# A blocked delta-rule recurrence on one core: two heads kept in halves of the partitions

## The chip, the cores and the metric

The kernel is one program on one core of a Trainium2 chip. The time is that of the device, in microseconds, from the start of the program to its end. TensorE (PE, with its weight loads as PEld), VectorE (DVE), ScalarE (ACT), GpSimd (POOL) and SyncE (SP) run their own instruction streams and meet at semaphores.

## What is computed

Two layers of a block with an RWKV-like recurrence, a convolution branch and a retrieval of experts (PEER), over 256 tokens of 1024 channels and a context of 256 tokens, then a second block of four attention-like branches and an MLP. All numbers are fp32. The change touches the recurrence alone, 16 heads of 64 channels, run forward and backward:

```python
def step(S, inp):
    w_t, k_t, v_t, kk_t, a_t = inp[:5]
    sa = jnp.einsum('bhvk,bhk->bhv', S, kk_t)
    S = (S * w_t[:, :, None, :]
         - sa[..., None] * (kk_t * a_t)[:, :, None, :]
         + v_t[..., None] * k_t[:, :, None, :])
    y = jnp.einsum('bhvk,bhk->bhv', S, inp[5]) if emit else None
    return S, y
S, ys = lax.scan(step, s0, xs, reverse=reverse)
```

It runs four times: on the context and on x in layer 0, on the context in layer 1 (where `emit` is false: states only, no y), on x in layer 1.

## The kernel before, in words

`first_block` calls `token_mixer` four times, and each calls `rwkv`. `rwkv` splits the 16 heads into four quarters of four heads and runs two sweeps over each, which makes eight units, `rwkv_unit`. A unit holds both halves i of the tokens (128 each); in sweep 0 half 0 goes forward and half 1 backward, in sweep 1 the other way round. The 256 tokens are cut into four chunks of 64, so each half has two chunks and its state passes through them in turn (n = 0, 1). Where `hh` counts the two heads of one tile of 128 channels, head hh owns 64 of the partitions.

A unit has three stages, parted by `k.phase()`, behind which engines wait for the counts of the stage before.

- Operands and grams. VectorE makes kt and rt (lines 642, 646) from exponentials that were made during the unit before. TensorE transposes V, kh and nb (677, 685). ScalarE copies V, then kt and rt into `rhs4` with the other head's channels zeroed (663), then the transposed kh and nb. TensorE multiplies kh and nb with the whole of `rhs4`, 512 columns at a time (705, 706), and `rhs4` with nb (708), four times; VectorE cuts each product into triangles with masks (725 to 731): MT, LdT, NT, ArT, AbT, Ld, each 128x128 a head with two chunks on the diagonal.
- The inverse, `invert_unit_lower`: 14 steps over two groups g of four 128x128 matrices. A step is eight matmuls (499; 497 for transposes); VectorE copies or adds the product out (459, 461), ScalarE copies for group 1, and for both groups while experts are hosted (479). A step of TensorE waits for the copy of the step before in its group. At step 9 the next unit's low-rank products (533, 534) and sigmoids (544, 545) are let in.
- The sweep over chunks. For n = 0, 1 and both halves i: Y and R from the state and from V (840, 841, 844), ScalarE copies R (778); S starts as identity times state plus khT times V (849, 852); U is TT times R (857), ScalarE copies U (783); S takes nbT times U (864) and VectorE writes the state as S times pc, masked to the two heads' blocks (811). After n = 0 ScalarE makes the next unit's exponentials (573 to 579). VectorE's queue holds in between the next unit's sums (554 to 565), rates (587 to 595) and scaled operands (602, 604). At the end Y takes ArT times V and AbT times U (872, 873), and VectorE adds it out (821).

The order of each engine is that of the code; there is no scheduler. `use_rows(k, dve, n)` (1206, 1210) sets n rows of an expert job into VectorE's queue, and `fetch_rows` the gathers for them on GpSimd (1226), in a ring of four; they do nothing while no job is hosted. A row is 128 tokens' own 1024 numbers each, half a megabyte. Rows of a job that are not used up in hosts are done in `finish_experts`, first in a loop with the same ring, then in full gathers (1438, 1443).

```python
HOSTED_CONTEXT, HOSTED_FIRST, HOSTED_LAST = 336, 240, 0
```

## Time and profile before

| | us |
|---|---|
| median of 3 runs (lowest, highest) | 7127.55 (7110.72, 7147.01) |
| profiled execution, span | 7128.6 |
| TensorE busy | 4259.3 |
| VectorE busy | 4001.5 |
| ScalarE busy | 1106.6 |
| GpSimd busy | 1826.1 |
| mean granted TensorE clock | 0.786 |

The profiled execution's own time is its span, 7128.6 us; it lies between the lowest and the highest of the timed runs and 1.1 us from their median. Busy times are shares of one span, so engines overlap; a row's mean time is a duration with the pipeline's depth in it, and what a stream of matmuls costs is read from the distance of their starts. A granted clock of 1.00 is 2.4 GHz, 0.50 is 1.2 GHz.

### The profile page before, as it was taken

What the parts mean: (1) busy time and instruction counts of PE and PEld (TensorE: products, weight loads), DVE (VectorE), ACT (ScalarE), POOL (GpSimd) and SP (SyncE); (2) the same over time, 40 slices, a digit from 0 to 9 for tenths busy, and PEclk for the clock granted to TensorE, in tenths of its full rate; (3) what the DMA queues carried; (4) which work ended last, traced back from release to release, by engine and by line L of the source; (5) the groups of instructions that cost most, each with busy time, mean ns of one, the idle gap of its engine ahead of it and who ended that gap; (6) DMA issues with size and microseconds to landing.
All of it is one profiled execution on the core that took longest, in us unless ns stands there. A gap on an engine that the chain in (4) does not pass through costs nothing. (4 is left out here: it accounts for less than half of the span.)

```text
span 7128.6 us, 68862 instructions
## 1 busy us (share of the span) xinstructions
PE 4259.3 (60%) x23168; PEld 3557.4 (50%) x23168; DVE 4001.5 (56%) x7384; ACT 1106.6 (16%) x2134; POOL 1826.1 (26%) x1546
## 2 busy tenths in 40 slices
PE   8777998568788730458881048798850000165788
PEld 1566776457576620347771037677740000154677
DVE  0345454375777777467778952555438888624210
ACT  0112221111323200113230001222110000011110
POOL 0000000022344357014446730000005877500000
PEclk9888998779899865778885579899975555576899
DMA  7230001256455588136658953100026999620233
GB/s 300 96 100 24 1 1 33 86 201 250 147 184 183 163 315 309 65 135 198 197 191 317 368 207 119 33 1 1 30 77 220 335 352 357 246 74 14 89 119 117
DMA packets 295477, 1114.93 MB, mean 156 GB/s; under 512 B 33313, under 2 KB 38705, under 8 KB 290097
## 3 DMA queue, kind: packets, MB, share of 16 engines
q0 software_dynamic: 221184, 805.40, 32.1%
q1 hardware_dynamic: 74032, 306.07, 12.4%
q8 instruction: 162, 2.65, 0.1%
q14 instruction: 99, 0.80, 0.0%
HBM read 1110.29 MB, written 1.05 MB: 156 GB/s over the span
## 5 line engine op out<-in xcount | busy, mean ns | idle before, releaser
L153 PE MATMUL psum<-h,weight_ring 128*128 128x256 f32 x5440 | 1219.6, 388 | 145.5 <-PEq L79 134.1
L153 PEld LDWEIGHTS psum<-h,weight_ring 128*128 128x128 f32 x5440 | 1060.4, 195 | 304.7 <-issue 140.0
L1226 POOL DMA_INDIRECT ring<-in_peer_u,expert x496 | 588.1, 1186 | 2335.4 <-SPq L79 1278.1
L1443 DVE SCALAR_TENSOR_TENSOR tok<-ring,act,tok 128x1024 f32<-128x1024 f32 x688 | 884.1, 1285 | 117.4 <-DMA ring<-in_peer_v,expert_group 81.1
L1479 PE MATMUL psum<-constants,tok 128*128 128x128 f32 x48 | 10.8, 421 | 1526.3 <-PEq L79 1526.3
L1395 POOL DMA_INDIRECT ring<-in_peer_v,expert_group x688 | 791.0, 1150 | 240.1 <-issue 217.2
L1479 PEld LDWEIGHTS psum<-constants,tok 128*128 128x128 f32 x48 | 9.8, 227 | 1527.1 <-issue 1527.1
L1206 DVE CUSTOM_DVE_ANT_0 ring<-ring,tok 128x1024 f32<-128x1024 f32 x496 | 592.7, 1222 | 162.2 <-DMA ring<-in_peer_u,expert 144.7
L1395 POOL DMA_INDIRECT ring<-in_peer_u,expert_group x272 | 344.6, 1267 | 1232.0 <-DVE expert_group L1431 1152.8
L1438 DVE CUSTOM_DVE_ANT_0 ring<-ring,tok 128x1024 f32<-128x1024 f32 x272 | 330.0, 1226 | 89.6 <-DMA ring<-in_peer_u,expert_group 86.5
L401 PE MATMUL psum<-squares,constants 128*128 128x256 f32 x246 | 86.3, 525 | 220.5 <-ACT squares L383 220.5
L153 PE MATMUL psum<-m,weight_ring 128*128 128x256 f32 x768 | 179.9, 399 | 53.1 <-PEq L79 53.1
L479 ACT ACTIVATE rhs<-psum 128x512 f32<-128x512 f32 x192 | 114.6, 597 | 548.9 <-PE psum L499 548.5
L153 PEld LDWEIGHTS psum<-m,weight_ring 128*128 128x128 f32 x768 | 154.5, 202 | 78.5 <-issue 55.3
L499 PE MATMUL psum<-rhs 128*128 128x128 f32 x1536 | 190.3, 280 | 0.0
L401 PEld LDWEIGHTS psum<-squares,constants 128*128 128x128 f32 x246 | 65.3, 273 | 240.3 <-ACT squares L383 226.9
L272 PE MATMUL psum<-ada_ring,c 128*2 128x512 f32 x384 | 166.9, 598 | 23.6 <-DMA ada_ring<-in_ada_w 23.6
L499 PEld LDWEIGHTS psum<-rhs 128*128 128x128 f32 x1536 | 179.1, 191 | 3.5
L461 DVE TENSOR_TENSOR TT<-psum,TT 128x512 f32<-128x512 f32 x198 | 133.5, 689 | 79.5 <-PE psum L499 79.5
L383 ACT ACTIVATE squares<-x_tokens 128x2048 f32<-128x2048 f32 x7 | 13.4, 1910 | 1060.8 <-PEq L79 1060.8
L705 PE MATMUL psum<-rhs,scaled 128*128 128x512 f32 (+1 forms) x256 | 138.9, 628 | 57.7 <-ACT rhs L663 53.7
L844 PE MATMUL psum<-V,MT 128*128 128x64 f32 x1024 | 163.7, 289 | 0.0
(490 smaller groups left out, 8077.8 us busy)
## 6 DMA issues: line engine op xcount, KB each, us to landing
weight_ring<-in_w_in SPq DMA_DIRECT2D x228, 512.0 KB
ada_ring<-in_ada_w SPq DMA_DIRECT2D x24, 2048.0 KB
weight_ring<-in_w_q SPq DMA_DIRECT2D x48, 512.0 KB
weight_ring<-in_w_out SPq DMA_DIRECT2D x32, 512.0 KB
weight_ring<-in_w_gate SPq DMA_DIRECT2D x32, 512.0 KB
weight_ring<-in_w_mlp_in SPq DMA_DIRECT2D x32, 512.0 KB
weight_ring<-in_w_mlp_out SPq DMA_DIRECT2D x8, 2048.0 KB
weight_ring<-in_w_oB SPq DMA_DIRECT2D x24, 512.0 KB
```

The lines of the kernel that those rows point to most:

```text
L153: mm = pe.matmul(k.bank(slot, tokens), ring[:, slot, j * P:j * P + P], rhs(j), start=(j == 0), stop=(j == w.kt - 1))
L272: mm = pe.matmul(k.bank(slot)[0:2, :], c[:, j, :], ring[:, slot, 512 * j:512 * j + 512], start=(j == 0), stop=(j == 7))
L401: mm = pe.matmul(total, k.ones, squares[:, j, :], start=(j == 0), stop=(j == tiles - 1))
L461: ins = dve.tensor_tensor(grp(out, g), product(q, g), grp(added, g), ALU.add)
L499: mm = pe.matmul(out, grp(left, g)[:, h, :], grp(right, g)[:, h, :], start=True, stop=True)
L705: pe.matmul(three[0][:, 0:width], kh, rhs, start=True, stop=True)
L844: mm = pe.matmul(bR[i][:, 64 * h:64 * h + 64], b.MT[:, i, h, :], b.V[:, i, 64 * h:64 * h + 64], start=False, stop=True, skip_group_check=True)
L1206: ins = dve.tensor_tensor_reduce(row, row, job.tok[:, tile, :], 1.0, 0.0, ALU.mult, ALU.add, dot)
L1226: pool.indirect_dma_start(job.ring[:, r % HOSTED, :], None, job.tables[kind], bass.IndirectOffsetOnAxis(ap=job.eidx[:, number:number + 1], ...
L1395: pool.indirect_dma_start(r.ring[:, j, :], None, table, bass.IndirectOffsetOnAxis(ap=idx8[part][:, j:j + 1], axis=0),).then_inc(k.gathered ...
L1438: dve.tensor_tensor_reduce(r.ring[:, j, :], r.ring[:, j, :], job.tok[:, tile, :], 1.0, 0.0, ALU.mult, ALU.add, r.dot8[:, part, j:j + 1]).t ...
L1443: dve.scalar_tensor_tensor(job.tok[:, tile, :], r.ring[:, j, :], r.act8[:, part, j:j + 1], job.tok[:, tile, :], ALU.mult, ALU.add).then_in ...
```

## The change

Each head stays in its half of the partitions. nb and kh of a chunk stand side by side in one tile C (nb first in head 0's partitions, kh first in head 1's), kt and rt in one tile KR. One gram product of 64 partitions by 128 columns for each head and chunk gives what four blocks gave before. A product of 64x64 gives Ld. V and U stand in one tile W, one in each half, so that one matmul with G replaces the two with MT and V, or with ArT, V, AbT and U. States are 64 columns wide instead of 128, without zero blocks. `Sp`, the decayed state, is made by ScalarE; VectorE adds S times pc to it. Y of a chunk is made in PSUM after S, both chunks are evacuated once, at the unit's end. The grams stay in PSUM banks 0 to 3 and are masked into G by VectorE between the first four steps of the inverse (`keep_grams`); the inverse uses banks 6, 7, 4 and 5. TensorE's first step of the inverse waits for group g's LdT and for the copy of CT, no more for the end of a whole stage. V is transposed in sweep 0 only. One call of `use_rows(k, dve, 1)` in the gram stage is gone. In the first unit of each `rwkv` GpSimd clears Ld, LdT, NT and W. The table of constants has four masks of 128 columns more.

The lines of the unit that are new or changed (the lines that they replace are in the listing above; those of chunks, waits and counts that only follow are left out):

```diff
+            if between is not None:
+                between(q, dve)
...
+                if q == 0 and banks_read is not None:
+                    pe.wait_ge(k.act_step.sem, banks_read[g])
...
+        for hh in range(2):
+            rows = slice(64 * hh, 64 * hh + 64)
+            for name, t, slot in (("nb", b.a, hh), ("kh", b.kd, 1 - hh)):
+                by_chunk = [x[rows].rearrange("p j (c t) -> p j c t", c=4) for x in (t, b.eN)]
+                chain(dve.tensor_tensor(b.C[rows, :, :, slot, :], by_chunk[0], by_chunk[1], ALU.mult))
...
+    def chunk(i, n):
+        return 2 * i + (n if ways[i] == 0 else 1 - n)
...
+            if sweep == 0:
+                act.wait_ge(k.multiplied.sem, k.multiplied.at(turned_v + 1))
+                for hh in range(2):
+                    act.activation(b.W[half(1 - hh), :, :, hh, :], k.bank(hh)[half(1 - hh)].rearrange("p (c j v) -> p c j v", c=4, j=2), ACT.Copy
+                                   ).then_inc(k.act_step.up(), 1)
...
+            dve.tensor_tensor(KR[:, 0], kk, b.eX, ALU.mult).then_inc(k.vec_step.up(), 1)
...
+                dve.tensor_tensor(KR[:, 1], operands.tiles(b.z), b.eP, ALU.mult).then_inc(k.vec_step.up(), 1)
...
+            dve.wait_ge(k.multiplied.sem, k.multiplied.at(lower + 1))
+            for i in range(2):
+                for hh in range(2):
+                    h = half(hh)
+                    dve.tensor_tensor(b.Ld[h, i, :, h], k.bank(4 + hh)[h, 256 * i:256 * i + 256].rearrange("p (n t) -> p n t", n=4),
+                                      masked(back[ways[i]][h, h], 4), ALU.mult).then_inc(k.vec_step.up(), 1)
+            for i in range(2):
+                dve.wait_ge(k.multiplied.sem, k.multiplied.at(grams + i + 1))
+                g = [k.bank(2 * i + hh).rearrange("p (n t) -> p n t", n=4) for hh in range(2)]
+                for out, mask in ((b.LdT, near), (b.NT, far)):
+                    for hh in range(2):
+                        h = half(hh)
+                        dve.tensor_tensor(out[h, i, :, h], g[hh][h, :, 0:64], masked(mask[ways[i]][h, h], 4), ALU.mult).then_inc(k.vec_step.up(), 1)
+                    if out is b.LdT:
+                        marks["ready", i] = k.vec_step.count
+                if i == 0:
+                    use_rows(k, dve, 1)
...
+            if sweep == 0:
+                for c in range(4):
+                    for j in range(2):
+                        for hh in range(2):
+                            at = (2 * c + j) * 64
+                            mm = pe.matmul(k.bank(hh)[half(1 - hh), at:at + 64], vz[half(hh), j, 64 * c:64 * c + 64], k.ident[half(hh), half(hh)],
+                                           start=True, stop=True)
...
+                for n in range(2):
+                    for j in range(2):
+                        at = (2 * n + j) * P
+                        mm = pe.transpose(k.bank(6 + i)[:, at:at + P], b.C[:, j, 2 * i + n].rearrange("p s t -> p (s t)"), k.ident)
...
+            for i in range(2):
+                for n in range(2):
+                    for j in range(2):
+                        c, at = 2 * i + n, 256 * i + (2 * n + j) * 64
+                        for hh in range(2):
+                            h = half(hh)
+                            mm = pe.matmul(k.bank(4 + hh)[h, at:at + 64], KR[h, 0, j, 64 * c:64 * c + 64], b.C[h, j, c, hh, :], start=True, stop=True)
...
+            for i in range(2):
+                for n in range(2):
                     for j in range(2):
...
+                        c, at = 2 * i + n, (2 * n + j) * P
+                        for hh in range(2):
+                            h = half(hh)
+                            rhs = KR[h, 0:2, j, 64 * c:64 * c + 64] if emit else KR[h, 0, j, 64 * c:64 * c + 64]
+                            out = k.bank(2 * i + hh)[:, at:at + cols]
+                            if emit:
+                                out = out.rearrange("p (a t) -> p a t", a=2)
+                            mm = pe.matmul(out, b.C[h, j, c].rearrange("p s t -> p (s t)"), rhs, start=True, stop=True)
...
+        def keep_grams(q, dve):
+            if q < 4:
+                i, hh = q // 2, q % 2
+                dve.tensor_tensor(b.G[:, hh, i, :, 0:cols], k.bank(2 * i + hh).rearrange("p (n t) -> p n t", n=4)[:, :, 0:cols],
+                                  masked(k.gram_mask[ways[i]][hh][:, 0:cols], 4), ALU.mult).then_inc(k.vec_step.up(), 1)
...
+                    for j in range(2):
+                        c = chunk(i, n)
+                        ins = act.activation(b.Sp[:, i, j], state(n, i)[:, j], ACT.Copy, scale=operands.pc[:, j, c:c + 1])
+                    ins.then_inc(k.act_step.up(), 1)
+                    marks["Sp", n, i] = k.act_step.count
...
+                        c = chunk(i, n)
+                        ins = dve.scalar_tensor_tensor(state(n + 1, i)[:, j] if n == 0 else states[i][:, j], k.bank(2 * i)[:, 64 * j:64 * j + 64],
+                                                       operands.pc[:, j, c:c + 1], b.Sp[:, i, j], ALU.mult, ALU.add)
+                    ins.then_inc(k.vec_step.up(), 1)
...
+                            h, at = half(hh), 64 * j
+                            pe.matmul(k.bank(2 * i + hh)[h, at:at + 64], KR[h, 0, j, 64 * c:64 * c + 64], state(n, i)[h, j], start=(j == 0), stop=False,
+                                      skip_group_check=True)
+                    for j in range(2):
+                        for hh in range(2):
+                            h, at = half(hh), 64 * j
+                            mm = pe.matmul(k.bank(2 * i + hh)[h, at:at + 64], b.G[:, hh, i, 2 * (c % 2) + j, 0:64], W[:, c, j, hh, :], start=False, stop=True,
+                                           skip_group_check=True)
...
+                        for hh in range(2):
+                            h, at = half(hh), 64 * j
+                            mm = pe.matmul(k.bank(2 * i)[h, at:at + 64], b.CT[:, c, j, h], W[:, c, j, hh, :], start=True, stop=True)
...
+                for i in range(2 if emit else 0):
+                    c = chunk(i, n)
+                    r = half(c % 2)
+                    for j in range(2):
+                        for hh in range(2):
+                            h, at = half(hh), P * i + 64 * j
+                            pe.matmul(k.bank(4 + hh)[r, at:at + 64], KR[h, 1, j, 64 * c:64 * c + 64], state(n, i)[h, j], start=(j == 0), stop=False,
+                                      skip_group_check=True)
+                    for j in range(2):
+                        for hh in range(2):
+                            at = P * i + 64 * j
+                            mm = pe.matmul(k.bank(4 + hh)[r, at:at + 64], b.G[:, hh, i, 2 * (c % 2) + j, 64:128], W[:, c, j, hh, :], start=False, stop=True,
+                                           skip_group_check=True)
...
+            u = buffers(k, inner, tot=[2, 2, 4], pc=[2, 2, 4], KR=[2, 2, 256], C=[2, 4, 2, 64], CT=[4, 2, P], G=[2, 2, 4, P], W=[4, 2, 2, 64],
+                        R=[2, 2, 64], S=[2, 2, 64], Sp=[2, 2, 64], LdT=[2, 4, P], NT=[2, 4, P], Ld=[2, 4, P], E1=[2, 4, P], E2=[2, 4, P],
+                        X=[2, 4, P], TT=[2, 4, P])
```

TensorE's stream in the operands and grams of an even unit, before (`scaled` holds kh and nb, `rhs_50` is rhs4):

```order
L677 MATMUL psum<-constants,z 128x128 x4
L685 MATMUL psum<-constants,scaled 128x128 x8
L692 UNCONDITIONAL_BRANCH
L705 MATMUL psum<-rhs_50,scaled 128x512
L706 MATMUL psum<-rhs_50,scaled 128x512
L708 MATMUL psum<-scaled,rhs_50 128x128 x2
```

And now:

```order
L729 MATMUL psum<-constants,z 64x64 x16
L738 MATMUL psum<-constants,C 128x128 x8
L748 MATMUL psum<-C,KR 64x64 x16
L764 MATMUL psum<-KR,C 128x128 x16
L491 UNCONDITIONAL_BRANCH
```

The three gram lines stood there four times, behind ScalarE's copies; now V takes 16 small matmuls (even units alone), and grams follow straight on the transposes.

TensorE's stream in one chunk of the sweep, before, from its start to the next chunk (the first three rows stand there four times, the next two twice):

```order
L840 MATMUL psum<-state,rt 128x128
L841 MATMUL psum<-state,kt 128x128
L844 MATMUL psum<-V,MT 128x64 x2
...
L849 MATMUL psum<-state,constants 128x256
L852 MATMUL psum<-V,khT 128x128 x2
...
L857 MATMUL psum<-rhs_50,TT 128x64 x8
L864 MATMUL psum<-rhs_50,nbT 128x128 x4
```

And now:

```order
L883 MATMUL psum<-state,KR 64x64 x4
L888 MATMUL psum<-W,G 64x64 x4
L883 MATMUL psum<-state,KR 64x64 x4
L888 MATMUL psum<-W,G 64x64 x4
L896 MATMUL psum<-R,TT 128x64 x4
L904 MATMUL psum<-W,CT 64x64 x8
L912 MATMUL psum<-state,KR 64x64 x4
L917 MATMUL psum<-W,G 64x64 x4
L912 MATMUL psum<-state,KR 64x64 x4
L917 MATMUL psum<-W,G 64x64 x4
```

Y moved behind S, the identity product is gone, and U has half the matmuls.

VectorE's stream from the last masks into the inverse, now (LdT and NT of the second half of the tokens, then X, copies, and G between them):

```order
L709 TENSOR_TENSOR LdT<-psum,constants 64x4x64 x2
L709 TENSOR_TENSOR NT<-psum,constants 64x4x64 x2
L443 UNCONDITIONAL_BRANCH
L454 TENSOR_TENSOR X<-Ld,constants 128x512 x2
L464 COPY E_49<-psum 128x512
L773 TENSOR_TENSOR G<-psum,constants 128x512
L464 COPY E_50<-psum 128x512
L773 TENSOR_TENSOR G<-psum,constants 128x512
```

Before, 24 masks of 128x256 stood ahead of X and no G behind it.

## Rows read from the trace of the kernel before

**Rows 1.** The page: its span, and a group of its part 5.
```profile
span 7128.6 us, 68862 instructions
...
L1206 DVE CUSTOM_DVE_ANT_0 ring<-ring,tok 128x1024 f32<-128x1024 f32 x496 | 592.7, 1222 | 162.2 <-DMA ring<-in_peer_u,expert 144.7
```

**Rows 2.** Busy time by stretch, the recurrence's four runs; first line names the columns.
```profile
core 0: us, PE busy (x) PEld busy (x) DVE busy (x) ACT busy (x) POOL busy (x), PEclk, DMA share, GB/s
603.70:1168.00 564.30, 512.24 (x3530) 436.38 (x3528) 276.57 (x566) 143.63 (x290) 0.00 (x0) 0.95 0.00 1
1822.70:2464.50 641.80, 527.13 (x3530) 456.84 (x3528) 489.70 (x887) 187.59 (x363) 270.96 (x224) 0.91 0.57 183
3201.00:3778.00 577.00, 485.28 (x3145) 435.86 (x3143) 422.78 (x798) 172.49 (x338) 258.31 (x214) 0.84 0.60 195
4535.90:5097.20 561.30, 510.28 (x3530) 435.61 (x3528) 276.38 (x565) 143.53 (x289) 0.00 (x0) 0.95 0.00 1
```

**Rows 3.** The same view: stretches of unit 1, first run (operands, grams, inverse, sweep).
```profile
675.00:678.80 3.80, 1.50 (x12) 1.28 (x12) 1.38 (x2) 3.12 (x6) 0.00 (x0) 1.00 0.00 0
678.80:691.90 13.10, 10.84 (x33) 5.83 (x33) 8.35 (x25) 0.89 (x2) 0.00 (x0) 0.87 0.00 0
691.90:723.10 31.20, 30.18 (x234) 28.48 (x235) 14.58 (x22) 8.72 (x18) 0.00 (x0) 0.95 0.00 1
723.10:746.20 23.10, 22.01 (x169) 19.60 (x168) 10.94 (x26) 6.05 (x13) 0.00 (x0) 1.00 0.00 1
```

**Rows 4.** Timeline, TensorE, grams: start, duration, instruction, idle before and its releaser.
```profile
678.87 1.43 PE L705 MATMUL psum<-rhs,scaled 128*128 128x512 f32 x2 [2.35 <-ACT rhs L663]
...
688.26 1.02 PE L706 MATMUL psum<-rhs,scaled 128*128 128x512 f32 x2
689.12 0.61 PE L708 MATMUL psum<-scaled,rhs 128*128 128x128 f32 x4
```

**Rows 5.** Timeline, VectorE, the last masks and X.
```profile
691.10 0.41 DVE L730 TENSOR_TENSOR AbT<-psum,constants 128x256 f32<-128x256 f32 x1
691.43 0.41 DVE L731 TENSOR_TENSOR Ld<-psum,constants 128x256 f32<-128x256 f32 x1
691.88 1.29 DVE L448 TENSOR_TENSOR X<-Ld,constants 128x512 f32<-128x512 f32 x2
```

**Rows 6.** Timeline, TensorE, from S to U in the sweep over chunks.
```profile
655.84 0.71 PE L852 MATMUL psum<-V,khT 64*128 64x128 f32 x4
656.47 0.70 PE L849 MATMUL psum<-state,constants 128*128 128x256 f32 x2
657.10 0.71 PE L852 MATMUL psum<-V,khT 64*128 64x128 f32 x4
657.74 2.00 PE L857 MATMUL psum<-rhs,TT 128*128 128x64 f32 x16
659.67 1.25 PE L864 MATMUL psum<-rhs,nbT 64*128 64x128 f32 x8
```

**Rows 7.** Timeline, TensorE, the transposes of the modulation, two columns each.
```profile
191.61 8.17 PE L300 MATMUL psum<-constants,ada_rows 2*128 2x2 f32 x96 [1.08 <-PEq L79]
```

**Rows 8.** Timeline, TensorE, low-rank products at step 9 and what follows them.
```profile
641.08 0.48 PE L533 MATMUL psum<-z,w 64*128 64x128 f32 x2
...
641.63 0.49 PE L533 MATMUL psum<-z,w 64*128 64x128 f32 x4
...
642.72 0.38 PE L499 MATMUL psum<-scaled,Ld 128*128 128x128 f32 x1
```

**Rows 9.** Timeline, ScalarE, the copy of R.
```profile
653.73 0.38 ACT L778 ACTIVATE rhs<-psum 128x256 f32<-128x256 f32 x1 [7.97 <-PE psum L844]
```

**Rows 10.** Busy time by stretch, third run: from TensorE's idle time to the unit's end.
```profile
3328.20:3346.00 17.80, 14.64 (x59) 12.78 (x60) 9.69 (x20) 2.22 (x7) 8.06 (x7) 0.50 0.71 233
```

**Rows 11.** The same view: first stage and sweep, third run; sweep, second run.
```profile
3274.10:3285.90 11.80, 8.55 (x44) 7.40 (x44) 10.85 (x26) 2.79 (x5) 4.50 (x4) 0.88 0.47 143
3318.70:3347.50 28.80, 23.49 (x121) 20.18 (x121) 19.81 (x39) 5.57 (x12) 13.13 (x10) 0.67 0.63 204
1953.80:1984.00 30.20, 24.62 (x168) 22.21 (x167) 23.53 (x47) 6.10 (x13) 14.47 (x11) 0.89 0.62 195
```

**Rows 12.** Waits in the second run's sweep: who for whom, total, times, longest.
```profile
PE psum L840 <- DVE state L811: 4.7, 1, 4.7
```

247 lines of the change are left out of this document (96 added, 151 removed).

## The prediction

> **What bounds the kernel now.** I read the page's head first: 7128.6 us, one core, so every gain has to come out of a chain on that core [rows 1]. Then the stretches by part of the program: the recurrence runs four times, in eight units each, over 564.3, 641.8, 577.0 and 561.3 us, or 70.5, 80.2, 72.1 and 70.2 us a unit [rows 2]. That is 2344 us, a third of the span; the rest (GEMMs, expert gathers, second block) keeps its code. The four parts are of three kinds: A (first and last, 16 units: no rows of experts ride along), B (second, 8 units, VectorE works on gathered rows too), C (third, 8 units, also with rows, no output Y).
>
> Inside a unit of kind A there are three stages [rows 3]: operands and grams, 3.8 + 13.1 = 16.9 us; the inverse, 31.2; the sweep over chunks, 23.1. In the last two TensorE is busy 30.2 of 31.2 and 22.0 of 23.1 us, so they are priced in matmuls. The first is not: TensorE waits 2.35 us for ScalarE's masked copies [rows 4], then VectorE masks 24 blocks at 0.33 us each, 8.0 us, and TensorE's last gram is long over when the first matmul of the inverse can start [rows 5].
>
> Two habits of the trace matter. Each fp32 matmul of the code is two MATMUL rows, a transpose is one. And a pair of LDWEIGHTS and MATMUL takes 0.12 us for 128 weights columns whether 128 or 64 columns stream: 16 rows of line 857 stream 64 and take 1.93 us [rows 6]; two of 512 columns take 0.43 us each [rows 4].
>
> **The change, part by part (kind A).** *Grams.* Removed: 8 rows of 512 columns, 8 of 128, the four ScalarE copies that made the zero-padded operand, 24 masks. Added: 16 matmuls of 64x64 (32 rows) for Ld, 16 of 64x128 (32 rows), in even sweeps 16 of 64x64 for V in place of 4 transposes. The trace of before has no 64x64 matmul, so I bound a row of one. Above: 0.12 us, like line 857, if narrow weights are no cheaper. Below: half the width would be 0.056 us; the narrowest that exists, 96 rows of two streamed columns, take 8.17 us, 0.085 each, more than half of it at half clock [rows 7]. I take 0.06. For 64 rows of contraction there is a row that speaks: lines 533 and 534 issue 16 MATMULs for one half of the partitions and then the other, and where the halves meet four rows of line 533 take 0.49 us, as two did before; all 16 and the change of shape behind them take 1.64 us, where 16 x 0.112 would be 1.79 [rows 8]. So matmuls on different partition halves run side by side, and the change alternates halves. The gram rows (128 weights columns, 64 partitions) therefore also go at 0.06 instead of 0.12. Each change of shape costs: line 849 after 852 starts 0.63 us after it, for 4 rows of 0.11, so 0.2 us are lost [rows 6].
>
> TensorE in an odd sweep: 8 transposes 0.9, 32 x 0.06 = 1.9, again 1.9, two changes 0.4: 5.1 us; even sweeps 2.1 more. VectorE: kt and rt, then 4 masks for Ld, 8 for LdT and NT, at 0.33 = 4.0, then X, 1.3 [rows 5]. Line 454 stands behind all masks in VectorE's queue, and behind it the copy of the first product for which TensorE's second step waits. 3.2 (lower products) + 0.2 + 4.0 + 1.3 + 0.7 = 9.4 us after the unit's start; 9.4 less the 1.9 of the first step gives an effective 7.5 us for the stage, 9.6 in even sweeps, mean 8.6. Against 16.9 that is **-8.3**; at half clock the transposes and the grams are slower, **-6.9**.
>
> *Inverse.* The same 14 steps. VectorE gets four maskings of 512 columns (0.69 each) in the first four steps; from step three it adds on the path as well, **+0.5**. A granted 0.95 over 31.2 us [rows 3] means that 1.6 us of it are already lost to 1.2 GHz; if the clock comes in low, I add as much again, **+1.7**.
>
> *Sweep over chunks.* Per chunk TensorE had 32 + 4 + 8 + 16 + 8 rows and at the end 32 more. Now: R 32, U 8, S 16, Y 32, at 0.06 except U at 0.11, with ten changes of shape: 5.7 + 2.0 = 7.7 us. Two waits open in it: U of the second half waits for ScalarE's R (0.9 us), S waits for U, which ScalarE copies only after four new activations for Sp (four of 0.22, from its 0.38 us for 256 columns, pitch lower [rows 9]); together 1.5. Y runs while VectorE updates S and hides that. 9.2 us a chunk, 18.4, then the single Y evacuation 1.1 and 0.4 between units: 19.9 against 23.1, **-3.2**. At half clock: R 3.6, wait 0.9, U 0.85, S with its wait 1.8, Y 3.6: 10.8 a chunk, 23.1 in all, **0**.
>
> *Which clock.* In kind C the granted clock fell to 0.50 after an idle time in the sweep and stayed there through 17.8 us in which TensorE was busy for 14.6 [rows 10]; this was half clock, 1.2 GHz, under a busy engine. The new sweep has idle spots of the same sort in every chunk, so I give half clock the larger share. Full clock gives -8.3 + 0.5 - 3.2 = -11.0, half -6.9 + 0.5 + 1.7 = -4.7; I take -7.5 a unit, **-120 us** for 16.
>
> The Trainium skill says this as a rule ("TensorE: Matmul & The Clock Gate", part 1): the default is the throttled clock, and activity releases it. It also says ("TensorEngine Tiling (Array Packing)", Key Properties) that tiles load and multiply in parallel, and that a change of tiling mode drains the engine; the 0.2 us above agree with the drain. [...]
>
> *Kind B.* First stage as in A, -8, of which VectorE's now shorter queue takes care. Inverse: VectorE has in the first five steps X, four G, four adds and five rows at 1.2 [rows 1]: 13.2 us against 9.7 of matmuls, less what the idle head absorbs, +2.5. Sweep: 30.2 us now with VectorE busy 23.5, TensorE waiting 4.7 us once for the state [rows 11, 12]. Four copies into Y go (0.4 each, as line 731), two extra C products come (0.65 each, as line 448), and the second chunk, which runs at half clock now, has fewer columns: 25.2, -5.0. Sum -10.5, 8 units, -84. One row of experts fewer is used per unit (27, not 28): eight move into the GEMM behind, half hidden, +7. **-77**.
>
> *Kind C.* First stage 11.8 us [rows 11], without a copy of rt, to 8.4, -3.4, inverse +1.0, sweep 28.8 [rows 11] to 21.4, -7.4: -9.8, -78. Eight rows of experts drop out of the units into the loop before the full gathers, at an estimated 1.8 us each (1.2 of VectorE and a wait for the ring), +14. **-64**.
>
> Clearing four tiles on GpSimd (hidden, 1 us) and a constants table of 0.26 MB more: **+6**. Sum: -120 - 77 - 64 + 6 = -255; 7128.6 - 255 = 6874, and the span stands 1 us above the median of the runs. I say **6875**.
>
> **Rivals.** (1) *Full clock, halves overlap everywhere*: A -11 (-176), B -11 (-81 with the moved rows), C -10.5 (-70), +6: 6808; with some overlap of output halves too, 6790. For it: rows 8. Against: rows 10. 20%. (2) *The gain is given back to waits and clock*: A -4.7 (-75), hosted units wait for gathered rows, whose ring of four does not shrink with the unit, B -5 (-33), C -5 (-26): 7000. 20%. (3) *Slower*: small matmuls run one after another and at 1.2 GHz, 0.107 us a row. A chunk is then R 4.3, 0.9, U 0.85 and a wait, S 2.4, Y 4.6: 13.5, the sweep 28.5 (+5.4); the first stage is 12.5 and 16.2, -2.5; inverse +2.5: +5.4 x 16 = +86, B -3 (-17), C -4.5 (-22), +6: 7181. It decides from about 0.09 us a row. Against it: rows 8, and the weights columns halved. 7%. (4) *It doesn't do what it says*: the grams' masks on VectorE hold the inverse back as much as the old ones; 7090, 3%.
>
> **How the numbers follow.** Forecast 50%, its own range 6830 to 6930. The range for 8 in 10 reaches from rival 1 to rival 2: 6780 to 7010. A measurement can tell 0.5% (36 us) from no change. Faster by more: forecast, rivals 1 and 2, and half of 4: 0.91; within: 0.02; slower: 0.07.
>
> **What would show it.** Right: a unit of kind A at 62 to 64 us; the first stage 8 to 10 us in odd sweeps and 2 more in even ones; rows of 64x64 at 0.06 us or side by side; 0.50 granted in part of the sweep and until the inverse has run some us; the second inverse step waiting for VectorE's copy behind G; B's sweep near 25. Wrong: pitches of 0.107 in the sweep (rival 3), 1.00 granted throughout (rival 1), gathered rows waited for longer than now (rival 2).

## The result, and the profile after

| | before | after |
|---|---|---|
| median of 4 runs (lowest, highest), us | 7119.1 (7110.2, 7147.0) | 6769.1 (6768.3, 6790.0) |
| profiled execution, span | 7128.6 | 6767.7 |
| four runs of the recurrence | 2344.4 | 1929.5 |
| the rest of the span | 4784.2 | 4838.2 |

The ratio is 0.950, 95% interval 0.948 to 0.952. That is 106 us under the forecast and 11 us under the low end of its range. The recurrence gave 415 us, and 54 came back outside it.

Busy time by stretch, after, the four runs of the recurrence (the columns are those of [rows 2], which they answer), then stages of unit 1 of the first run: first stage, inverse, sweep (they answer [rows 3]), then the sweep of unit 2, and last that of unit 3 of run 4 (units are counted from 0):

```profile
603.10:1050.00 446.90, 387.71 (x3920) 345.32 (x3920) 261.71 (x483) 151.75 (x384) 0.00 (x0) 0.91 0.01 1
1695.80:2219.00 523.20, 404.77 (x3920) 365.61 (x3920) 437.22 (x776) 196.27 (x458) 236.59 (x195) 0.84 0.62 195
2988.50:3497.00 508.50, 369.06 (x3408) 336.39 (x3407) 426.45 (x796) 191.03 (x449) 249.47 (x207) 0.80 0.67 213
4279.60:4730.50 450.90, 392.79 (x3920) 350.52 (x3920) 261.88 (x483) 151.87 (x384) 0.00 (x0) 0.90 0.01 1
...
661.40:666.30 4.90, 4.13 (x72) 3.72 (x72) 3.83 (x8) 1.09 (x2) 0.00 (x0) 1.00 0.00 0
666.30:700.00 33.70, 30.30 (x232) 28.05 (x232) 19.27 (x31) 8.72 (x18) 0.00 (x0) 0.95 0.00 1
700.00:716.00 16.00, 12.79 (x176) 10.44 (x176) 10.48 (x23) 9.53 (x29) 0.00 (x0) 0.89 0.00 1
...
754.90:773.60 18.70, 16.35 (x176) 13.66 (x176) 10.69 (x23) 9.54 (x29) 0.00 (x0) 0.63 0.00 1
...
4490.40:4504.90 14.50, 11.39 (x176) 9.24 (x176) 10.41 (x23) 9.53 (x29) 0.00 (x0) 1.00 0.00 1
```

A unit fell by 14.7, 14.8, 8.6 and 13.8 us in the four runs. In runs 1 and 4 the sweep's length goes with the granted clock: 14.5 us at 1.00, 16.0 at 0.89, 18.7 at 0.63. The table has means over the eight units of a run, each stage taken from the start of line 686 (642 before), of the first matmul of line 509 (499) and of line 883 (841; where y is made, line 840 starts some 0.3 us ahead of it before, which so counts with the inverse):

| us | first stage | inverse | sweep |
|---|---|---|---|
| run 1 | 16.8 → 5.8 | 30.7 → 32.5 | 22.7 → 17.1 |
| run 2 | 17.0 → 7.1 | 33.0 → 35.2 | 29.5 → 22.3 |
| run 3 | 12.2 → 7.3 | 31.5 → 34.9 | 28.1 → 21.0 |
| run 4 | 16.6 → 6.1 | 30.5 → 32.9 | 22.7 → 17.0 |

Timeline of TensorE, after, unit 1: first stage, then part of the sweep (start, duration, instruction, idle before it and its releaser):

```profile
661.42 1.06 PE L738 MATMUL psum<-constants,C 128*128 128x128 f32 x8 [1.19 <-PEq L79]
662.41 1.15 PE L748 MATMUL psum<-C,KR 64*64 64x64 f32 x32
663.49 2.06 PE L764 MATMUL psum<-KR,C 64*128 64x128 f32 x32
666.35 0.82 PE L509 MATMUL psum<-Ld,LdT 128*128 128x128 f32 x5 [0.81 <-DVE LdT L709]
```

```profile
708.30 0.45 PE L883 MATMUL psum<-S,KR 64*64 64x64 f32 x8
708.68 0.45 PE L888 MATMUL psum<-W,G 128*64 128x64 f32 x8
...
709.82 1.38 PE L896 MATMUL psum<-R,TT 128*128 128x64 f32 x8
712.21 1.03 PE L904 MATMUL psum<-W,CT 128*64 128x64 f32 x16 [1.01 <-ACT W L830]
713.17 0.45 PE L912 MATMUL psum<-S,KR 64*64 64x64 f32 x8
713.55 0.68 PE L917 MATMUL psum<-W,G 128*64 128x64 f32 x8
714.16 0.45 PE L912 MATMUL psum<-S,KR 64*64 64x64 f32 x8
```

They answer [rows 4] and [rows 6]. Read from start to start, 32 rows of line 748 take 1.08 us, 0.03 a row with the change of shape in it, where I had taken 0.06. Eight rows of line 883 and the change to line 888 take 0.38 us together; by the forecast they would have taken 0.68.

VectorE behind the masks ([rows 5]), and TensorE's weight loads of the inverse's first two steps:

```profile
669.05 1.29 DVE L454 TENSOR_TENSOR X<-Ld,constants 128x512 f32<-128x512 f32 x2
670.37 0.69 DVE L464 COPY E<-psum 128x512 f32<-128x512 f32 x1
670.98 0.68 DVE L773 TENSOR_TENSOR G<-psum,constants 128x512 f32<-128x512 f32 x1
```

```profile
668.83 0.30 PEld L509 LDWEIGHTS psum<-Ld,LdT 128*128 128x128 f32 x2
671.12 2.21 PEld L509 LDWEIGHTS psum<-LdT,Ld 128*128 128x128 f32 x10 [1.99 <-DVE E L464]
```

The second step waits for a copy that stands behind X, 9.7 us after the unit's start; the forecast had 9.4.

Busy time by stretch outside the recurrence: behind runs 2 and 3, after, then the same two of the kernel before:

```profile
2219.00:2988.50 769.50, 248.39 (x1089) 210.56 (x1090) 538.61 (x931) 56.94 (x102) 286.94 (x255) 0.65 0.58 212
3497.00:4279.60 782.60, 277.55 (x1217) 238.80 (x1218) 482.51 (x627) 64.74 (x118) 320.19 (x286) 0.67 0.65 234
```

```profile
2464.50:3201.00 736.50, 240.95 (x1065) 204.80 (x1066) 501.39 (x899) 56.16 (x101) 268.68 (x222) 0.66 0.56 201
3778.00:4535.90 757.90, 275.80 (x1192) 237.40 (x1193) 471.08 (x608) 63.96 (x117) 305.50 (x274) 0.68 0.65 235
```

They are 33 and 25 us longer, with 32 and 19 more instructions on VectorE. Counting the starts of lines 1248 and 1252, the units of run 2 use 27, 27, 27, 27, 27, 27, **6** and 27 expert rows (28 each before), and 75 rows are left behind it (46 before). 88 rows are used ahead of run 2, 88 + 6 x 27 = 250, and the rows of the second kind are not let in before all 256 of the first have been used and their weights are made, which happens between units only. So unit 14 hosts the last six and no more. Run 3 hosts 26 a unit and leaves 10 rows (27 and 2 before).

### The profile page after: what moved, and what is told of

Its sections match the earlier page's. It is cut to its first block and busy times, and to the rows that moved or that the text cites. A ratio compares the mean times of both kernels' runs of the same rounds, so it can differ in the third digit from the quotient of the medians.

```text
span 6767.7 us, 72149 instructions
## 1 busy us (share of the span) xinstructions
PE 3779.0 (56%) x24704; PEld 3191.6 (47%) x24704; DVE 3974.9 (59%) x7160; ACT 1153.8 (17%) x2534; POOL 1834.1 (27%) x1562
## 3 DMA queue, kind: packets, MB, share of 16 engines
HBM read 1110.55 MB, written 1.05 MB: 164 GB/s over the span
## 5 line engine op out<-in xcount | busy, mean ns | idle before, releaser
L509 PE MATMUL psum<-E,E 128*128 128x128 f32 x1584 | 199.3, 283 | 0.0
L509 PEld LDWEIGHTS psum<-E,E 128*128 128x128 f32 x1584 | 188.6, 194 | 3.7
L486 ACT ACTIVATE E<-psum 128x512 f32<-128x512 f32 x198 | 118.3, 597 | 403.7 <-PE psum L509 403.4
```

Of the source, the lines that this page charges most:

```text
L486: act.activation(grp(out, g), product(q, g), ACT.Copy).then_inc(k.act_step.up(), 1)
L509: mm = pe.matmul(out, grp(left, g)[:, h, :], grp(right, g)[:, h, :], start=True, stop=True)
```

## The experiments

Each was compared with the kernel before, run beside it on the same chip; its median was 7115.7 to 7132.7 us. So ratios are compared, and gains in us against the changed kernel are differences of the ratio from 0.950 times 7120. The intervals reach some 0.002 (14 us) to both sides, and so does that of the 0.950: a difference of less than about 20 us, as in e9 and e10 or between e4 and e12, shows nothing. e1 and e5 ran once each and are read for their bursts alone.

| | ratio (95%) | against the changed kernel, us |
|---|---|---|
| e2 one head first, everywhere | 0.957 (0.955 to 0.959) | +51 |
| e3 28 rows | 0.947 (0.945 to 0.948) | −24 |
| e4 X later | 0.946 (0.945 to 0.948) | −28 |
| e6 one head first for both chunks, sweep | 0.978 (0.976 to 0.979) | +196 |
| e7 before, 27 rows | 1.004 (1.002 to 1.006) | |
| e8 G first | 0.969 (0.968 to 0.971) | +137 |
| e9 24 rows | 0.952 (0.950 to 0.954) | +13 |
| e10 one start | 0.951 (0.949 to 0.954) | +9 |
| e11 filler | 0.943 (0.940 to 0.945) | −53 |
| e12 24 rows, X later, G later | 0.945 (0.942 to 0.948) | −37 |
| e13 e6 with the filler | 0.962 (0.960 to 0.964) | +86 |
| e14 V turned twice | 0.953 (0.951 to 0.955) | +23 |
| e15 filler, X later | 0.942 (0.940 to 0.944) | −57 |
| e16 filler, X later, 28 rows | 0.940 (0.938 to 0.941) | −73 |

### What a small matmul costs (e1, e5)

```diff
+    def part(rows, cols, bank, width=64):
+        def one(pe, at):
+            return pe.matmul(k.bank(bank)[cols, at * width:at * width + width], k.ident[rows, cols], x[rows, at, 0:width], start=True, stop=True)
```

> The changed kernel with one more stage ahead of the first layer: ten bursts of 24 matmuls (48 rows, since each fp32 matmul shows as two rows), each with 24 dense 128x128 ones of 128 columns ahead of it, the series run twice. Bursts: (1) 128x128 by 128 columns, (2) 128x128 by 64 columns, (3) 64x64 in one quadrant, (4) 64x64 in the two diagonal quadrants by turns, (5) 64x64 with the same rows and the halves of the output by turns, (6) 64x64 in all four quadrants, (7) 128x64 to one half of the output, (8) 128x64 to both halves by turns, (9) 64x128 from one half of the rows, (10) 64x128 from both by turns. Theory 1 (halves of the array work beside each other, and this made a row of the changed sweep 0.03 us where the forecast had 0.06): burst 3 takes 48 x 0.055 = 2.6 us or a little less, burst 4 about 48 x 0.03 = 1.4 us. Theory 2 (a narrow matmul with 64 columns is cheap by itself, and alternation gives nothing): bursts 2, 3 and 4 all take about 1.4 us, half of burst 1. Bursts 5 to 10 say which kinds of halves overlap; theory 1 expects 4 and 6 alike.

Busy time by stretch, one burst of 48 rows each (the first columns are length, TensorE and its weight loads; then the granted clock): 128x128 with 64 columns moved, 64x64 in one quadrant, two diagonal quadrants by turns, four quadrants, 128x64 to one half of the output, to both by turns:

```profile
35.80:41.30 5.50, 5.50 (x50) 5.38 (x49) 0.00 (x0) 0.00 (x0) 0.00 (x0) 1.00 0.01 3
41.30:44.20 2.90, 2.90 (x49) 2.87 (x48) 0.00 (x0) 0.00 (x0) 0.00 (x0) 1.00 0.00 0
49.80:51.30 1.50, 1.50 (x49) 1.47 (x48) 0.00 (x0) 0.00 (x0) 0.00 (x0) 1.00 0.00 0
...
64.00:64.80 0.80, 0.80 (x49) 0.79 (x48) 0.00 (x0) 0.00 (x0) 0.00 (x0) 1.00 0.00 0
70.40:73.30 2.90, 2.90 (x49) 2.87 (x48) 0.00 (x0) 0.00 (x0) 0.00 (x0) 1.00 0.00 0
78.90:80.40 1.50, 1.50 (x49) 1.48 (x48) 0.00 (x0) 0.00 (x0) 0.00 (x0) 1.00 0.00 0
```

Fewer moved columns gain nothing (5.50, where the dense matmuls of 128 columns between the bursts take 5.56), 64 weight columns in place of 128 halve a row (2.9), and halves by turns halve it again (1.5). Theory 1 holds, theory 2 falls. It doesn't matter whether the halves are of the rows, of the output or of both. Four quadrants take 0.86 us up to the next burst, a little more than a quarter of one quadrant's 2.9. The Trainium skill ("TensorEngine Tiling (Array Packing)", Key Properties) says that different tiles load weights and multiply in parallel, and this agrees. Two halves by turns give 0.03 us a row, half of what the forecast took.

> As the first experiment, with twelve other bursts of 24 matmuls (48 rows): the two diagonal 64x64 quadrants by turns of one matmul (a), of two (b), of four (c), of twelve (d); the same by turns of one into one PSUM bank (e); 128x64 by turns to the two halves of the output of one bank (f) and of two banks (g); 64x64 from the two halves of the rows to the same half of the output (h); 64x128 from the two halves of the rows (i); 128x64 with 128 moving columns to the two halves (j); 128x128 and 128x64 by turns of four (k) and of one (l). The sweep of the second experiment kept 0.034 us a row although it took two matmuls of one head before two of the other, while the grams, sixteen rows of a head before sixteen of the other, went from 0.030 to 0.054. Theory 1 (the halves overlap, a few matmuls ahead are looked at): a, b near 1.55 us, c between, d near 2.9. L904 alternates halves in one bank at 0.054 us a row: if the bank is why, f takes 2.6 to 2.9 and g 1.55; if not, both 1.55. k and l give the price of a change of shape: l minus the sum of its rows, over 23 changes, 0.1 to 0.2 us each.

The same view: by turns of one matmul (a), two (b), four (c), twelve (d), then 64x128 from two halves of the rows (i) and turns of four between 128x128 and 128x64 (k):

```profile
19.01:20.55 1.54, 1.54 (x49) 1.48 (x48) 0.00 (x0) 0.00 (x0) 0.00 (x0) 1.00 0.00 0
26.11:27.70 1.59, 1.59 (x49) 1.52 (x48) 0.00 (x0) 0.00 (x0) 0.00 (x0) 1.00 0.00 0
33.26:35.30 2.04, 2.04 (x49) 1.97 (x48) 0.00 (x0) 0.00 (x0) 0.00 (x0) 1.00 0.00 0
40.86:43.62 2.76, 2.76 (x50) 2.69 (x49) 0.00 (x0) 0.00 (x0) 0.00 (x0) 1.00 0.00 0
...
77.58:80.40 2.82, 2.82 (x49) 2.75 (x48) 0.00 (x0) 0.00 (x0) 0.00 (x0) 1.00 0.02 6
...
94.19:99.02 4.83, 4.83 (x50) 4.42 (x49) 0.00 (x0) 0.00 (x0) 0.00 (x0) 1.00 0.00 0
```

Two matmuls of one half before two of the other overlap as well as one by one, four less, twelve hardly. One bank (e) or two give the same 1.55, so the bank was no cause; line 904's mean holds a wait between its two halves of the tokens. Its first eight rows start at 712.21, the other eight at 712.79, behind ScalarE's copy of W (712.19 to 712.74); by 0.03 us a row they would start at 712.45. A burst ends in one change of shape, so with 0.13 for that a row is 0.029 by turns (a) and 0.059 in one quadrant (e1); k has six changes: 4.83 - 24 x 0.112 - 24 x 0.059 = 0.73, 0.12 each. In the sweep, eight rows and a change take 0.38 = 8 x 0.030 + 0.14. The forecast had 0.2. l ran partly at half clock and is not read, and neither is e1's burst of 64x128 from one half of the rows: it took 7.6 and 7.7 us at a granted 0.71 and 0.69 in its two turns. TensorE was busy all through that one, so waits are not all that brings the clock down.

### Order and clock in the sweep (e2, e6, e11, e13)

e2 puts one head before the other within each product:

```diff
-                    for j in range(2):
-                        for hh in range(2):
+                    for hh in range(2):
+                        for j in range(2):
```

> The changed kernel with the matmuls of the grams and of the sweep in another order: all of the head in the lower half of the partitions, then all of the head in the upper half, instead of the two by turns. Nothing else differs. Theory 1 (overlap of the two halves of the array): the 32 gram rows of 64x64 go from 1.08 us to about 1.9, the 32 of L764 from 1.9 to up to 3.8 at full clock, 72 rows of the sweep by 0.03 us more each and block and head pair: a unit of run 1 longer by 2 to 5 us, the kernel by 60 to 150 us. Theory 2 (the width alone): the same time within 10 us.

Its grams, in an odd unit of run 4:

```profile
4606.81 1.90 PE L748 MATMUL psum<-C,KR 64*64 64x64 f32 x32
4608.63 2.82 PE L764 MATMUL psum<-KR,C 64*128 64x128 f32 x32
```

Line 748 went from 1.15 to 1.90 us as theory 1 has it, line 764 from 2.06 to 2.82, less than expected. The mean sweep of run 1 stayed (17.3 for 17.1): there a turn is two matmuls, which e5 shows to be free. The expectation had missed that, and the 51 us in all lie under its 60 to 150. e6 makes the turns longer:

```diff
-                for i in range(2):
-                    c = chunk(i, n)
+                for hh in range(2):
+                    h = half(hh)
+                    for i in range(2):
+                        c = chunk(i, n)
```

> The changed kernel with the sweep's products of the lower head for both chunks (16 rows) ahead of those of the upper head, in the R and in the Y products; the grams and the rest as they were. Theory 1 (overlap of halves made the sweep short too): 32 rows of a step go from 1.53 to about 1.9 us at 2.4 GHz for R, and 0.3 longer for the state's rows of Y, so 1 to 1.4 us a unit, 30 to 45 us in all, 6800 to 6815. Theory 2 (the sweep is short by its fewer rows and waits alone): within 10 us of the changed kernel.

The sweep of run 1 became 24.9 us, 7.7 longer, not 1.4, and the granted clock 0.65 (0.79 in the changed kernel). TensorE in the sweep of unit 5: in the middle of the first chunk's Y the clock falls to 1.2 GHz, and stays there to the sweep's end.

```profile
975.13 0.45 PE L917 MATMUL psum<-W,G 128*64 128x64 f32 x4
975.51 0.69 PE L913 MATMUL psum<-state,KR 64*64 64x64 f32 x4
```

So two things were mixed. e11 holds the clock, by one dense matmul where TensorE waits for W; nothing uses its result:

```diff
+                pe.matmul(k.bank(6), k.ident, k.segments, start=True, stop=True)
                 for i in range(2):
                     c = chunk(i, n)
                     pe.wait_ge(k.act_step.sem, marks["U", n, i])
```

> The changed kernel with one more matmul (128x128 by 512 columns, into a free bank, 0.9 us at 2.4 GHz) in each of the sweep's two steps, where TensorE waits 1.01 us for the scalar engine's copy of W. Nothing that is computed uses it. Clock theory (the sweep's half-clock stretches, 0.79 of 2.4 GHz granted on average in run 1 where before had 1.00, come from TensorE's small tiles and waits; dense work there holds the clock): sweeps of 18.7 us become 16, up to 1.3 us a unit on average, 20 to 40 us shorter, 6730 to 6750. Rival (the wait is on the path, the filler ends late and the clock falls all the same): 0 to 0.3 us longer a step, 0 to 25 us longer.

The sweep of runs 1 and 4 became 14.7 us at a granted 0.99, and those runs 429 and 428 us long in place of 447 and 451. In runs 2 and 3 the clock rose in the sweep too (0.71 to 0.79, 0.62 to 0.70) but its length stayed. VectorE's expert rows set it there: in e9, with a row fewer in each of the two steps, the sweeps of run 3 are 19.2 us long with the time to the next unit, and 21.8 in the changed kernel. The filler fits into the wait: from the start of line 896 to that of the S products are 2.36 us with it (698.73 to 701.09 in unit 1) and 2.37 without (701.60 to 703.97). So all of the 2.4 us that the mean sweep lost is the clock, and the changed kernel's own sweeps at 1.00 (14.5 us) say the same. The Trainium skill ("TensorE: Matmul & The Clock Gate", part 1) says that activity releases the full clock; this row agrees. e13 is e6 with the filler:

> The sixth experiment (lower head's products ahead of the upper head's in the sweep) with the eleventh's filler matmul in each step. The sixth had sweeps of 24.9 us at a granted clock of 0.65 in run 1, against 17.1 at 0.79 of the changed kernel and 14.7 at 0.99 with the filler alone. Theory 1a (the lost overlap costs 1 to 2 us at full clock, and the clock made the rest): with the filler the sweep lasts 15.7 to 17 us at a clock above 0.9, and the time is 6750 to 6790. Theory 1b (the lost overlap itself costs most of the 7.7 us, at any clock): 20 us or more, the time above 6850. If the filler doesn't hold the clock here, the sweep stays near 24 us at 0.65, and the question stays open.

Sweep of unit 1 with both, then with the filler alone (busy time by stretch), and single groups of e13 and of e11 (timeline, TensorE):

```profile
700.90:719.40 18.50, 16.80 (x169) 12.43 (x168) 9.21 (x23) 9.52 (x29) 0.00 (x0) 1.00 0.00 1
```

```profile
697.10:711.20 14.10, 13.21 (x180) 9.69 (x180) 9.98 (x23) 9.52 (x29) 0.00 (x0) 1.00 0.00 1
```

```profile
706.20 0.44 PE L918 MATMUL psum<-W,G 128*64 128x64 f32 x4
706.57 0.44 PE L914 MATMUL psum<-state,KR 64*64 64x64 f32 x4
```

```profile
702.05 0.45 PE L913 MATMUL psum<-state,KR 64*64 64x64 f32 x8
702.43 0.68 PE L918 MATMUL psum<-W,G 128*64 128x64 f32 x8
```

At 1.00 granted, seven of the eight sweeps of run 1 last 19.5 us, against 14.6: 4.9 us for the order, between my 1a and 1b (the kernel's 6855 us lie on the side of 1b). It is made of groups: 32 of four rows at 0.37 (11.9 us) for 12 of eight rows at 0.38 and four of eight at 0.61 (7.0). Sixteen more changes of shape are 2.1 us of that, and 96 rows that no longer overlap 2.8. Over the whole kernel e13 is 86 + 53 = 139 us longer than e11, where e6 was 196 us longer than the changed kernel. The clock was held in run 1 alone, and that run is 34 us longer by the order, of 59 in e6. In runs 3 and 4 e13's sweeps had 0.60 and 0.92 granted, e11's 0.70 and 1.00. So the 139 still hold some clock, and the other 57 or so are the least of what the clock took.

### The first stage (e8, e10, e14, e4)

```diff
-                          following, (6, 7, 4, 5), [marks["ready", 0], marks["ready", 1]], keep_grams,
+                          following, (6, 7, 4, 5), [marks["G"], marks["G"]], None,
```

> The changed kernel with the masks of G ahead of the inverse on the vector engine, and the inverse waiting for them, in place of between its first copies. Forecast's theory (the first stage fell by what VectorE no longer did in it): the first stage of a unit longer by four masks, 2.5 to 2.8 us, of which 1 to 1.5 come back in the inverse, so 1 to 1.8 us a unit, 30 to 55 us in all, 6800 to 6825. Rival (the masks between the steps hold up the inverse by as much as they leave the first stage): within 10 us of the changed kernel.

The first stage of run 1 became 11.8 us (5.8), the inverse 31.2 (32.5), a unit 4.4 longer. TensorE, unit 3:

```profile
792.70 1.65 PE L509 MATMUL psum<-Ld,LdT 128*128 128x128 f32 x6 [6.04 <-DVE G L773]
```

I had overlooked that this edit also makes the first group wait for the masks of the second. e10 makes only that wait (`[marks["ready", 1], marks["ready", 1]]`):

> The changed kernel in which the inverse's first group waits for the masks of the second chunk pair too; G is still masked between the steps. The eighth experiment took both away at once and cost 137 us, 4.4 a unit of run 1, where I had expected 1 to 1.8 for G alone. If the start of the first group on its own masks is what carried it, this run costs 1.8 us (four masks at 0.45) in the first stage of a unit, with up to 0.9 given back in the inverse: 30 to 60 us in all, 6800 to 6830, and G in the first stage cost the other 80 to 100. If instead the clock's fall behind an idle TensorE carried it, this one costs less than 1 us a unit, under 30 us, and the half-clock stretch at the inverse's start is absent.

The first stage grew by 2.3 us, the inverse gave back 1.7, and a unit of run 1 stayed at 55.9. So the separate start is worth nothing there, and it is keeping G out of the first stage that is worth the 4.4 us. In runs 2 and 3 it is worth about 1 us a unit (8 and 10 us in the profiled executions). The kernel as a whole was 9 us longer, which is inside the error.

e14 turns V in both sweeps again:

> The changed kernel with V turned again in the backward sweep (16 more 64x64 matmuls and their copy on the scalar engine in every odd unit) in place of the reuse. The forecast had the first stage of an odd unit 2 us shorter than of an even one by the reuse; the trace shows 4.9 against 6.0 to 6.7 in run 1. So 1.1 to 1.8 us in 16 units: 18 to 29 us, 6785 to 6800. Rival (the copy delays the products behind it, or the clock rises by the extra work): outside 5 to 40 us.

The first stage of odd units went from 4.9 to 6.7 us in run 1, and the kernel was 23 us longer, both as expected. In run 4 it went from 5.4 to 6.0 only, and the run was no longer.

e4 takes X out from ahead of the first copies (`start()` is called behind the copies of step 0):

> The changed kernel with X = Ld + I of a unit issued on the vector engine behind the first step's copies of the inverse instead of ahead of them. The trace after shows TensorE's second step of the inverse waiting 1.99 us for the copy behind the masks and X. Theory of the forecast (the inverse became longer by a wait on the vector engine): the inverse shorter by 1 to 1.5 us in 32 units, 30 to 48 us in all, the time 6720 to 6740. Rival (TensorE has low-rank products to do then, or the wait goes to the next step): within 10 us of the changed kernel.

The inverse fell by 1.0 us in run 1 and 1.4 in run 4, and not at all in the hosted runs (35.2 and 34.9 as in the changed kernel): only the inverses of the 16 units of kind A gained by it, about 20 us. The runs as wholes did not share alike: run 1 fell by 3 us only, for its first stages were 0.7 us longer, and run 4 by 28, where the sweeps were also shorter (15.5 us for 17.0), by the clock.

### The expert rows (e3, e7, e9)

> The changed kernel with 28 expert rows hosted in a unit again instead of 27. Theory 3 (54 us of the gain in the units were given back behind them, by rows that stand alone after run 2 and run 3, because the 27 rows end six short of the 256 that the next kind of row waits for, so that unit 14 hosts 6 rows only): unit 14 hosts 28 or nearly, the rows left over fall from 75 to about 48, the time falls by 25 to 50 us, to 6720 to 6745. Rival (the later stages are longer for another reason, or rows cost as much inside a unit as outside): within 10 us of the changed kernel.

> The kernel before with one hosted expert row fewer in a unit (27), nothing else: this part of the change alone. Theory 3 (the row count alone gave back some 50 us behind the units, since unit 14 of 16 then hosts six rows only): the stretches behind run 2 and run 3 are 40 to 60 us longer; the units are shorter by the 2 to 3 us that a row costs in one (3.2 and 2.0 us between 27 and 28 in the third experiment), some 35; in all the time 5 to 30 us longer. Rival (the later stages are longer for another reason): they stay as long as before, and the time falls by 30 us or more.

> The changed kernel with 24 expert rows hosted in a unit in place of 27: none at the masks, one fewer in each of the sweep's two steps. 88 + 7 x 24 = 256, so the first kind of row ends with a unit, and run 2 hosts 280 rows where 27 in a unit gave 283. Theory 3 (the loss behind the units comes from unit 14 standing at the 256th row, and a row in a unit costs 2 to 3.2 us there, as between 27 and 28): units of run 2 and run 3 shorter by 3 x 2 to 3 us in 15 of them, 90 to 140 us, unit 14 longer by 18 rows, some 30; behind run 2 as before (78 rows alone for 75), behind run 3 24 rows more at 1.8 us, 43: in all 15 to 65 us shorter, 6705 to 6755. Rival (rows in a unit lie beside other work but for the one at the masks): units shorter by 2 to 3 us only, and with 24 rows more behind run 3 the time rises by 0 to 40 us.

The edits change the counts in `use_rows` alone. Lengths in the profiled executions, us:

| | run 2 | behind it (rows left) | run 3 | behind it (rows left) |
|---|---|---|---|---|
| before, 28 | 642 | 736 (46) | 577 | 758 (2) |
| e7, before, 27 | 620 | 776 (75) | 569 | 780 (11) |
| after, 27 | 523 | 769 (75) | 509 | 783 (10) |
| e3, 28 | 549 | 724 (46) | 525 | 769 (2) |
| e9, 24 | 502 | 791 (78) | 476 | 819 (34) |

e7 shows theory 3: 62 us more behind the two runs, 30 less in them, and 28 us longer in all. e3 takes 59 off behind and pays 42 in the units (its profiled execution is 40 us above its median, so these lengths are rough). So a row is dear in a unit too, and what is lost behind mostly comes back inside. e9 shortened the units by 21 and 33 us, less than the 90 to 140 expected, and lost as much behind them. That is 2.6 and 4.1 us a unit for three rows, nearer the rival's 2 to 3, and its +13 us is in the rival's range (0 to 40 longer).

### Together (e12, e15, e16)

> The changed kernel with three edits together: 24 hosted rows in a unit (ninth experiment), X behind the first step's copies (fourth, 31 us shorter), and G masked between steps 4 to 7 of the inverse in place of 0 to 3, the first of which wait for copies. If the gains add: 31 for X, 15 to 65 for the rows, 0 to 20 for G's place: 6650 to 6725. If X later and G later remove the same wait, only 6675 to 6740.

> The eleventh experiment (filler, 48 us shorter) and the fourth (X behind the first copies, 31 us shorter) together. If they touch different waits, 70 to 85 us shorter than the changed kernel, 6685 to 6700. Rival (part of the fourth's gain was the clock in run 4's sweeps, 15.5 us for 17.0, which the filler has already): 50 to 65 us shorter, 6705 to 6720.

> As the run before, with 28 hosted rows in a unit (third experiment, 20 us shorter: 29 fewer rows alone behind run 2, at 1.8 us, against 2 to 3 us more in each unit of runs 2 and 3). If it adds, 15 to 25 us shorter than the run before, 6660 to 6700; if X behind the copies takes longer beside a row more at the masks, the same time.

e12 is no better than e4 alone; which of its three parts took the gain back was not separated. In e15, X gained 1.5 us in a unit of runs 1 and 4 over e11 (52.1 for 53.6), some 23 us with the clock held. By the ratios the whole gained only 4 us, inside the error (17 between the profiled executions), and its 6709 us is what the rival had. e16 is the fastest kernel here, 6689.8 us, 6.0% under the kernel before, and in the range expected.

## Why the prediction fell short

The direction and the places were right, the gain was 106 us too small (255 forecast, 361 measured between the profiled executions). The step that failed is the price of a row of a small matmul: 0.06 us in the forecast, 0.03 in the runs, since narrow weights and halves by turns each halve it. By its own terms:

**Kind A, −120 forecast, −228 measured.** This term is 108 us off, as much as the whole forecast. That the others cancel is luck: B gained 35 more, C 9 less, the expert rows cost 37 more and the rest of the span 10 less. e11, with the clock held, sizes its two steps: a unit of kind A is 53.6 us there, 16.7 under the 70.3 of before, where the forecast's full-clock end was 11.0. Of that the clock took 2.5 us in the changed kernel; the forecast had put 3.5 on it. So of the 6.7 us a unit that were missed, 5.7 are prices at full clock and 1.0 is the clock:

- *The price of a 64x64 row (0.06 us) and of a change of shape (0.2) failed*, by 4.3 of the 5.7 us. e1 and e5 give 0.03 by turns and 0.13. In a chunk R takes 4 x 0.38 = 1.52 us where the forecast's terms give 2.72, and Y 2 x (0.38 + 0.61) = 1.98 for 2.72; the 16 rows of S, with the wait among them, 0.96 for 1.16. Twice these differences is 4.3 us. U with its waits, from its start to that of S, takes 2.36 us for 2.58, 0.4 in two chunks. Together they bring the forecast's 19.9 (with 0.4 between units) to 15.2, and the sweep at a held clock lasts 14.7, or 15.1 with the same 0.4. The wait for W stands where the forecast put it, behind ScalarE's four activations for Sp (710.52 to 711.58). I had read from [rows 8] that halves run side by side, and from the narrow weights that a row costs half, but had not multiplied the two: 0.06 is the price by either one alone. e13 is the check: with the turns broken, at full clock, a row is back at 0.06 and the sweep lasts 19.5. That this equals the forecast's 19.9 less 0.4 is partly chance, since e13 has more changes of shape and each is cheaper.
- *The weight of the half clock* was a smaller error. The clock did fall (0.79 in run 1's sweeps), but for stretches of a few us, and a sweep at a mean of 0.63 lasted 18.7 us, not up to 23.1: rows that overlap are short at 1.2 GHz too (eight rows of line 912 and the change, 0.62 us at 705.05).

First stage and inverse together gave 9.1 us in run 1 (47.5 to 38.4); the forecast had 7.8 at full and 5.2 at half clock. That is the rest of the 5.7. The second step's start was placed to 0.3 us, as a sum of errors: VectorE's masks are dearer than I had them (0.45 us for 64x256, from [rows 5] 0.33), the grams cheaper. V's rows in even units take 1.1 us, not 2.1.

**Kind B, −84 forecast, −119 measured.** First stage −9.8 (−8), inverse +2.2 (+2.5), sweep −7.2 (−5.0). By e7, 22 of the 119 us come from the expert row, which the forecast had not taken off the units; of kind C's 69 below it is 8.

**Kind C, −78 forecast, −69 measured.** First stage −4.9 (−3.4), sweep −7.1 (−7.4), but the inverse +3.5 (+1.0): as I read it, with rows in VectorE's queue G and X have no room there; e9, without the row at the masks, has an inverse of 33.3 us in run 3, for 34.9. The first stage shows the same as in A.

**Expert rows, +21 forecast.** Behind the units it was 58 us. That unit 14 would stop at row 250 could have been worked out from the count of 88 and the barrier at 256; I took one row a unit. With the 30 us that the units lose by it, the term as a whole is 28 (e7), so the sum was hardly wrong by it.

**+6 for clearing and constants.** The stretches ahead of run 1 and behind run 4 are within a few us of before; not measured by itself.

**Rivals.** Rival 1 (full clock, halves overlap everywhere, 6790 to 6808) was the nearest, and half of it happened: the halves overlap everywhere but in line 917, the clock was not full. It had 18 us for the overlap of output halves; e13 against e11 shows up to 139 for the order. Rival 3's 0.107 us a row occurs in line 917 alone, whose rows all go to one half of the output, and there in the half-clock stretches (1.05 us for eight and a change at 705.67); elsewhere rows were far under its deciding 0.09. Rival 2's waits for gathered rows did not grow (VectorE's in run 2: 22.6 + 7.6 = 30.2 us before, 19.1 + 7.5 = 26.6 after, with one row fewer in a unit). The range's low end, 6780, stood just under rival 1, and every case in it had rows of 0.056 us or more. That bound was one of the width alone.

Open: why stretches outside the recurrence differ by 10 us and more between kernels with the same rows left (behind run 1: 646 to 661 us). Not tried: the activations for Sp behind the copies of W, which TensorE waits for.

## What to carry to other kernels

Two facts that each halve a price may multiply: when both have a row of their own, take the product as the end of the range. Small matmuls pay when halves take turns every one or two matmuls (quadrants were run by turns of one alone) and shapes change seldom, and an order that looks the same can cost 200 us in 6770, in part by the clock. Where a count is spread over hosts ahead of a barrier, add it up to the barrier before moving one of it.

## What the runs showed of the hardware

- A row of fp32 with 64 columns moved costs 0.112 us for 128 weight columns, 0.059 for 64, 0.029 with two halves by turns, 0.015 with four quadrants, all at 2.4 GHz (e1). By turns between halves, 64x128 takes 0.056 and 128x64 with 128 columns moved 0.055 (e5, i and j).
- Turns of two matmuls overlap nearly as well as turns of one (48 rows in 1.59 and 1.54 us), turns of four less (2.04), of twelve hardly (2.76) (e5).
- A change of the matmul's shape costs 0.12 to 0.14 us (e5, k, and the sweep's groups).
- With fewer and shorter matmuls the granted clock of run 1's sweeps was 0.79, where the kernel before had 1.00. One dense matmul a chunk, put into a wait, brought it to 0.99, and was worth 53 us.
